# Sixteen bias-table loads moved from the end of a feed-forward block into the attention projection on the load queue

## The reference, cut to what matters

```
dr_idx = rs + jnp.arange(kr) - r + NA_ROWS - 1
bias = rpb[:, dr_idx][:, :, dc_idx].transpose(0, 2, 1, 3)
s = s + bias[None].astype(jnp.float32)
s = jnp.where(col_in[:, None, :], s, NEG_INF)
p = jax.nn.softmax(s.reshape(B_, H, GRID_W, kr * GRID_W), axis=-1)
```

## Time and profile before

| | |
|---|---|
| median of 3 runs | 1010.27 us |
| the profiled execution | 1010.27 us |
| its span in the trace | 1008.3 us |
| TensorE busy | 941.5 us (93%) |
| VectorE busy | 726.9 us (72%) |
| ScalarE busy | 434.3 us (43%) |
| read from DRAM | 237.54 MB, mean 237 GB/s |

### The profile page before, as it was taken

The page is one execution under the profiler, slowest core; times in us unless marked ns, Lnnn a source line. Parts: engine busy times, 40 slices in busy tenths (PEclk is TensorE's granted clock), DMA queues, the critical chain, the costliest instruction groups (busy, mean ns, idle before and its releaser), DMA issues.

```text
span 1008.3 us, 11291 instructions
## 1 busy us (share of the span) xinstructions
PE 941.5 (93%) x4368; PEld 769.4 (76%) x4368; DVE 726.9 (72%) x789; ACT 434.3 (43%) x555; POOL 105.3 (10%) x179
## 2 busy tenths in 40 slices
PE   4699999999998598999999999999999789999998
PEld 3588788787777466888888878888888668888876
DVE  4785988966879846888888677878784777654543
ACT  1543434344556546452434364343443464343431
POOL 2010111100502100011111000101110000000000
PEclk9699999999999789999999999999999989999999
DMA  9989998686943016999999458976894278656221
GB/s 340 379 288 375 373 320 282 229 231 169 373 168 125 0 45 216 347 311 344 327 332 318 155 186 301 331 250 214 292 311 161 86 232 299 200 168 208 84 82 44
DMA packets 147125, 239.34 MB, mean 237 GB/s; under 512 B 16128, under 2 KB 108160, under 8 KB 146944
## 3 DMA queue, kind: packets, MB, share of 16 engines
q1 hardware_dynamic: 126768, 167.01, 49.3%
q0 software_dynamic: 19440, 71.31, 20.3%
q10 hardware_dynamic: 864, 0.30, 0.1%
HBM read 237.54 MB, written 1.05 MB: 237 GB/s over the span
## 4 chain that ended last, share of the span: by engine, by line
PE 76%; DVE 10%; ACT 3%; issue 3%; DMA 3%; SPq 3%; POOL 1%; DVEq 0%; ACTq 0%
PE ps L1363 46%; PE ps L1420 7%; PE ps L1421 7%; PE ps L1424 7%; DMA raw<-in_ff_w 2%; SPq L389 2%; PE ps L1396 2%; DVE lo L873 1%; DVE xn L982 1%; PE ps L1435 1%; ACT arena L600 1%; PE ps L1455 1%; POOL rstd L496 1%; PE ps L1355 1%; DVE x L986 1%
## 5 line engine op out<-in xcount | busy, mean ns | idle before, releaser
L1363 PE MATMUL ps<-hi,hT_hi 128*128 128x512 f32 (+1 forms) x848 | 338.9, 400 | 8.5 <-DVE hT_lo L1001 4.8
L1363 PE MATMUL ps<-hi,hT_lo 128*128 128x512 f32 (+1 forms) x848 | 330.7, 390 | 0.0
L1363 PE MATMUL ps<-lo,hT_hi 128*128 128x512 f32 (+1 forms) x848 | 330.4, 390 | 0.0
L873 DVE TENSOR_TENSOR lo<-raw,hi 128x2048 fp32r<-128x2048 f32 (+1 forms) x76 | 171.5, 2261 | 37.2 <-ACT hi L576 37.0
L1363 PEld LDWEIGHTS ps<-hi,hT_hi 128*128 128x128 f32 x848 | 160.4, 189 | 46.8 <-issue 10.1
L1363 PEld LDWEIGHTS ps<-hi,hT_lo 128*128 128x128 f32 x848 | 160.3, 189 | 33.7
L1363 PEld LDWEIGHTS ps<-lo,hT_hi 128*128 128x128 f32 x848 | 160.6, 189 | 32.5 <-issue 1.4
L576 ACT ACTIVATE hi<-raw 128x2048 fp32r<-128x2048 f32 (+1 forms) x76 | 143.6, 1892 | 22.7 <-DMA raw<-in_ff_w 19.8
L479 POOL DMA_DIRECT2D ada<-in_ada_w x132 | 71.1, 539 | 502.7 <-DVE acc L925 192.6
L925 DVE SCALAR_TENSOR_TENSOR acc<-ada,cond,acc 128x1024 f32<-128x1024 f32 x73 | 93.6, 1282 | 7.7 <-DMA ada<-in_ada_w 3.9
L873 DVE TENSOR_TENSOR lo<-arena,hi 128x2048 fp32r<-128x2048 f32 x30 | 68.7, 2288 | 13.3 <-ACT hi L576 13.3
(11 more groups left out here) (162 smaller groups left out, 1070.8 us busy)
## 6 DMA issues: line engine op xcount, KB each, us to landing
raw<-in_ff_w SPq DMA_DIRECT2D x204, 512.0 KB, 5.5
ada<-in_ada_w POOLq DMA_DIRECT2D x132, 512.0 KB, 6.3
arena<-in_ff_w SPq DMA_DIRECT2D x60, 512.0 KB, 6.0
raw<-in_w_in SPq DMA_DIRECT2D x24, 512.0 KB, 4.9
arena<-in_ada_w SPq DMA_DIRECT2D x4, 1024.0 KB, 18.4
raw<-in_w_out SPq DMA_DIRECT2D x8, 512.0 KB, 4.5
raw<-in_ada_w SPq DMA_DIRECT2D x2, 1024.0 KB, 15.1
arena<-in_b_rpb SPq DMA_DIRECT2D x16, 128.0 KB, 4.5
```

Of the source, the lines that this page charges most:

```text
L873: ins = V.tensor_tensor(lo, src, hi.bitcast(F32), ALU.subtract)
L1363: ins = mm(out, a, b, start=first and m == 0, stop=last and m == len(pairs) - 1, skip_group_check=shared)
```

## The change

The sixteen bias loads leave the last two pairs of `ffn(0)`. They now stand in the loop over the mixer's pieces: after the pieces that `load_until(n)` issues, two bias loads follow, for n = 22 to 29. The wait for unit 16 stands once ahead of the loop. The loads themselves (addresses, sizes, destination) are the same.

```
-                    if f == 0 and p >= PAIRS - 2:
-                        sp.wait_ge(unit_used, last_in((4, 5), MIX_PIECES[0]) + 1)
-                        for i in range(2 * ROWS):
-                            load_bias(p - PAIRS + 2, i // ROWS, i % ROWS)
                 if f == 0:
+
+                    sp.wait_ge(unit_used, last_in((4, 5), MIX_PIECES[0]) + 1)
                     for n in MIX_PIECES:
                         load_until(n)
+                        for i in range(2 * (n - MIX_PIECES[0]), 2 * (n - MIX_PIECES[0]) + 2):
+                            if i < TT * 2 * ROWS:
+                                load_bias(i // (2 * ROWS), i // ROWS % 2, i % ROWS)
```

## The result

| | before | after |
|---|---|---|
| median of four runs each | 1010.58 us | 1017.12 us |
| ratio, 95% interval | | 1.0073 [1.0052, 1.0093] |
| the profiled execution, its span | 1010.27, 1008.3 us | 1016.09, 1014.0 us |

The change costs 0.73% where 0.14% was forecast, and the median lies above the range. The ratio is taken over more runs than the four of the medians (21 of the changed kernel, 1014.63 to 1020.75 us, median 1018.54), which is why it isn't their quotient of 1.0065. The page of the changed kernel hardly differs from the earlier trace rows: TensorE's share of the chain is one point higher, that of the DMAs too.

What follows compares the result with a forecast made beforehand. TensorE, busy 941.5 of 1008.3 us, was taken as the bound. Removal 0, piece 28 +1.4, pieces 27, 29 and the table 0, on 1010.27 us, gave 1011.7 us, with a range from 1009.7 to 1014.6.

Steps and rivals of the forecast that it cites:

- The removal: Bias loads leaving 215 to 250 us: costed at nothing, a gain of at most 0.82 us of TensorE's idle time.
- The path: Piece 28 lands late, ScalarE's high part, then VectorE's low part, then TensorE's 48 products; 1.4 us of loss.
- Its slack: Piece 28 may land as late as 273.2 without delaying VectorE's low part, which starts at 275.13; it landed at 270.1.
- The stretch of 276 to 280 is full: Sign expected in the changed profile: window 276 to 280 should be full of DMA.
- `bias_window` waits for nothing: Table needed at 313.75, last pair issued from about 289.6: over 20 us, no cost; late table given 0.03.
- The price of a pair on the DMA engines: Eight loads fill all 16 engines for 6.5 us, 0.81 us a load; 1.3 to 1.6 us for a pair.
- Piece 28 lands: Two pairs ahead, 3.2 us: lands at 273.3, or 274.6 to 275.3 with `ada` loads passing; 1.4 us late taken.
- The first rival: Backlog grows beyond one wait: 0.95 us a load, two `ada` loads passing, piece 28 at 276.6, time 1013.7; chance 0.33.
- So no piece is issued late: SyncE in the mixer's pieces: a pair takes 1.6 us to issue, done by about 253.1, piece 27 due at 253.36.
- Piece 27, "No cost": One pair and two `ada` loads ahead: lands at 263.2 to 265.9, its low part could start at 266.87; no cost.
- The small gain on the `ada` load: VectorE's 0.88 us wait at 261.29 might shrink by 0 to 0.5 us beside short bias runs; taken as 0.
- turns are by single runs: Two busy queues get 66 and 66 packets in 1 us, read as the engines alternating run by run.

Runs made afterwards that it cites:

- big_runs: Changed kernel with sixteen loads of the same 128 KB into the same 64 partitions, in 64 runs of 2 KB, not 512 of 256 bytes; 1.0074 to before.
- changed_again: The changed kernel once more, with no edit; 1.0046 [1.0030, 1.0061] to the kernel before.
- half_early: Changed kernel with only four pairs of bias loads, behind pieces 26 to 29, the other eight loads in their old place; 1.0076 to before.
- spread_source: Changed kernel with the 256-byte runs read from 64 distinct rows of w_in, not the 15 KB table, into the old destination; 1.0045 to before.
- every_second: Changed kernel with 128 KB loads of w_in in 512 runs of 256 bytes, written to the even or odd partitions instead of a half; 1.0025 to before.
- act_queue: Changed kernel with the bias loads issued in pairs by ScalarE on its own queue, behind its high part of pieces 25 to 32; 1.0031 to before.
- the probes: Two variants of the kernel before, its two groups of eight bias loads replaced by 128 KB loads of other widths and run lengths; ran once each, 208 to 306 GB/s.

## Why the prediction was wrong

The removal was priced right. TensorE is busy for 9.18 us of 240 to 250 in both kernels, the start of piece 26 moves by 0.4 us, and nothing before 250 had waited for the bias loads.

The path was right too: piece 28's landing, ScalarE's high part, VectorE's low part behind it instead of behind `qk_scale(0)`, TensorE. Its slack, a landing at 273.2, holds in the eight kernels that land later. The stretch of 276 to 280 is full (q1 at 104.7%), and `bias_window` waits for nothing, as said.

The step that failed is "The price of a pair on the DMA engines" together with what it was multiplied by, in "Piece 28 lands". It forecast a landing 4.5 us later than before (four loads at 0.81 and one `ada` load), at 273.3 to 275.3. It came 8.5 us later. Term by term:

| term | forecast | measured in the window |
|---|---|---|
| bias loads by piece 28's last landing | 4 | 6.0 |
| price of one | 0.81 us | 1.07 us |
| `ada` loads that pass | 1 (1.3 us) | 2 (2.6 us) |
| less of the later pieces moved | 0 | -0.5 us |
| sum | 4.5 us | 6.4 + 2.6 - 0.5 = 8.5 us |

The price of 1.07 is what is left once the others are counted, so the sum closes by its making; the number of loads and of `ada` loads are counted from packets. The price was read from a group that ran alone and was low. The misses seem to hang together: a later landing lets the next `ada` load pass, and the pair issued behind piece 28 is moved before piece 28 has wholly landed. That delay feeds delay in this way fits the packets; no run shows it by itself. The first rival had this mechanism ("the backlog grows") at 0.33; with 0.95 us a load it gave 1013.7, too little as well, since it too counted four loads.

More important than the size is what the earlier trace rows hid. They showed 4096 runs in 6.5 us, and I read them as "many short runs". The same row held the slow half: 1.10 MB in 6.5 us is 169 GB/s with all engines reported as busy. For loads alone the two halves of this weigh alike, 177 GB/s becoming 242 or 244. In company, which is what counted here, the width weighs more: going from 64 to all 128 partitions at the same length takes a load from 0.99 to 0.56 us, and making the runs eight times as long in 64 partitions only from about 1.0 (0.87 to 1.07) to 0.8.

"So no piece is issued late" was wrong: piece 28's issue takes 6.0 us and piece 29's begins 3.5 us late. By big_runs this isn't what makes piece 28 late. Piece 27, "No cost", landed at 269.3 instead of by 265.9; in changed_again it came at 265.8 with the same loss, so it cost nothing of its own. The small gain on the `ada` load, taken as 0, is a small loss: VectorE waits 1.43 us for it, 0.88 before. Nor does show that turns are by single runs: 66 packets of each queue in 1 us on 16 engines come out alike by any turns of equal length. So the rule that the prediction weighed there, from the Trainium skill ("DMA: Bandwidth & Descriptors", Queues, rings and completion order), that an engine drains a whole packet of descriptors before it switches, is neither borne out nor refuted here. By either rule the load would have come sooner, if anything, and it did not.

A term was missing altogether: TensorE's clock. The forecast moved TensorE's start and left its products at 11.2 us. After waits of 3 to 4 us they took 12.57 (12.72 again, 13.88 in big_runs, 14.03 in half_early), 1.35 us of the 6.8. In spread_source, where TensorE was busy for 1.97 of the 2.4 us ahead, the clock was 1.00 for them and the stage grew by the lateness alone; so it did in every_second. In spread_source it had fallen earlier, to 0.52 in 276 to 278, behind a wait for piece 27 (TensorE busy for 0.39 of the 2 us ahead), and was back at 1.00 from 280. It slowed products behind which TensorE had to wait for piece 28 anyway.

What stays open:
- Why a narrow load costs more in the later, less crowded stretch. From 280 to 300 q1 alone moves 4.85 MB in 20 us:

```profile
q1 hardware_dynamic: 5928, 4.85, 115.5%
```

  4033 packets are short, about 7.4 loads; the 3.88 MB of pieces take 9.7 us at 401 GB/s, so a load costs 1.4 us. This stretch no longer sets the end, and I didn't test it further.
- Why alternating halves in one queue helped so little.
- How the loss would split if SyncE weren't held while the runs stay short. act_queue takes that wait away only by putting it elsewhere, and takes the loads out of the pieces' queue at the same time.

## What to carry to other kernels

Price a load by the partitions that it writes and the length of its runs, not by its bytes: 128 KB into one half of the partitions cost 0.9 to 1.1 us of a full DMA system here in 256-byte runs and 0.8 in 2 KB runs, into all partitions 0.56 in 256-byte runs and 0.36 in 1 KB runs. Before putting such loads in front of others, count for the tightest of these the slack up to the last landing, and let every queue that is full at the time pass once more for each delay. Where TensorE then has to wait, look at its granted clock behind the wait too, which was worth 1.35 to 2.8 us in four profiles here and nothing that shows in the others. A table that must be narrow is best loaded where nobody queues behind it, as the kernel before did.

## What the runs showed of the hardware

- Loads into partitions 0 to 63 or 64 to 127 moved 177 GB/s (256-byte runs) to 244 GB/s (2 KB runs) with all 16 engines reported busy, loads into all of them 242 and 400.
- A DMA's issue can hold the engine that issues it: 0.42 us before, up to 5.6 us for one on SyncE (8.1 in spread_source) and 6.04 on ScalarE, with 512 short runs in each load ahead in that queue. With 2 KB runs the two DMAs of piece 28 were issued in 0.89 us, and so were those of piece 29.
- After 0.41 busy us in 3, TensorE's granted clock was 0.51 in the next 3 us and 0.92 in the 3 behind. After 3.2 us of nothing (big_runs) it was 0.50 in the next 5.8. After 1.97 busy us in 2.4 (spread_source) it was 1.00.
- GpSimd's first root (L496) took 5.0 us in eleven of fourteen kernels (the probes not counted), those in which VectorE's low part of piece 27 started beside it (268.79 and 268.88 before), and 2.93 us in the three others, in which piece 27 was late and VectorE waited (changed, spread_source, every_second). In the changed kernel this gained nothing, since piece 28 came later than the root.
